# Modulation rows made by GpSimd as per-partition sums in the first block, summed by TensorE in the second

## The reference

```python
x = x + 0.5 * swiglu(rms_norm(x, norm_ffn1[l]), ffn1_in[l], ffn1_out[l])
...
x = x + 0.5 * swiglu(rms_norm(x, norm_ffn2[l]), ffn2_in[l], ffn2_out[l])
```

```python
m = jax.nn.silu(c) @ mod_w[l] + mod_b[l]            # 1024 x 6144 weights, for both layers
sh1, sc1, g1, sh2, sc2, g2 = jnp.split(m[:, None, :], N_MOD, axis=-1)
h = rms_norm_2(x, norm1_g[l]) * (1.0 + sc1) + sh1
mc = jax.nn.silu(c_ctx) @ mod_w[l] + mod_b[l]       # used in layer 0 alone, its first 2 x 1024 columns
```

## Time and profile before

| what | us |
|---|---|
| median of 3 runs | 3894.78 |
| the profiled execution, its own time | 3896.48 |
| its span in the trace | 3894.4 |
| first up stage (22.9 to 155.9) | 133.0 |
| first down stage (155.9 to 220.9) | 65.0 |
| modulation stage (1917.6 to 2128.6) | 211.0 |

### The profile page before, as it was taken

One profiled execution on the slowest core, in us unless ns is written; L12 is line 12 of the kernel. 1 busy time (PEld: TensorE's weight loads), 2 busy tenths in 40 slices (PEclk: granted clock), 3 DMA queues, 4 the chain that ended last, 5 costly groups with the idle time before them and its releaser, 6 DMA issues. The chain is left out here.

```text
span 3894.4 us, 51801 instructions
## 1 busy us (share of the span) xinstructions
PE 3014.0 (77%) x18986; PEld 2115.1 (54%) x18986; DVE 2191.8 (56%) x4138; ACT 1255.4 (32%) x2479; POOL 629.4 (16%) x544
## 2 busy tenths in 40 slices
PE   7988682798998786479887687677777776777776
PEld 7887671697988576369633557322222262222222
DVE  5455755553545566555300545777777457777774
ACT  3332112332433210333211233344444323444443
POOL 0000000000000000000011000444444204444442
PEclk9999895899999898589999758899999988999999
DMA  6453000444545200144585303899999838999997
GB/s 211 149 178 124 2 5 30 148 160 152 189 141 179 95 2 8 49 157 151 205 297 205 106 6 115 331 421 421 421 421 419 334 119 367 421 421 421 421 419 308
DMA packets 274498, 849.81 MB, mean 218 GB/s; under 512 B 13528, under 2 KB 161136, under 8 KB 208240
## 3 DMA queue, kind: packets, MB, share of 16 engines
q0 software_dynamic: 73728, 536.90, 33.2%
q1 hardware_dynamic: 200560, 310.19, 23.7%
HBM read 846.00 MB, written 1.05 MB: 218 GB/s over the span
## 5 line engine op out<-in xcount | busy, mean ns | idle before, releaser
L595 DVE TENSOR_TENSOR weight_parts_lo<-raw_weights,weight_parts_hi 128x512 fp32r<-128x512 f32 (+7 forms) x224 | 497.2, 2243 | 340.1 <-ACT weight_parts_hi L571 340.1
L571 ACT CAST weight_parts_hi<-raw_weights 128x512 fp32r<-128x512 f32 (+7 forms) x224 | 409.2, 1861 | 417.0 <-PE banks L450 367.8
L2226 PE MATMUL banks<-raw_weights,diagonals 128*128 128x512 f32 x832 | 414.1, 636 | 152.1 <-ACT diagonals L184 151.0
L448 PE MATMUL banks<-normedT_hi,weight_parts_hi 128*128 128x256 f32 x1664 | 478.1, 287 | 20.2 <-DVE weight_parts_lo L595 20.2
L2226 PE MATMUL banks<-expert_rows,diagonals 128*128 128x512 f32 x816 | 395.7, 624 | 115.3 <-ACT diagonals L184 114.5
L449 PE MATMUL banks<-normedT_lo,weight_parts_hi 128*128 128x256 f32 x1664 | 476.9, 287 | 0.0
L450 PE MATMUL banks<-normedT_hi,weight_parts_lo 128*128 128x256 f32 x1664 | 476.8, 287 | 0.0
L2226 PEld LDWEIGHTS banks<-raw_weights,diagonals 128*128 128x128 f32 x832 | 154.9, 199 | 407.9 <-ACT diagonals L184 231.8
L1640 POOL TENSOR_TENSOR modulation<-modulation,mod_bias 128x512 f32<-128x512 f32 x24 | 30.3, 1264 | 2087.3 <-DMA mod_bias<-mod_b 1953.2
L2138 POOL DMA_INDIRECT raw_weights<-peer_rows,expert_ids x208 | 242.8, 1167 | 749.3 <-DVE expert_ids L151 468.0
L2226 PEld LDWEIGHTS banks<-expert_rows,diagonals 128*128 128x128 f32 x816 | 149.8, 195 | 358.9 <-ACT diagonals L184 224.1
(11 more groups left out here) (391 smaller groups left out, 5081.1 us busy)
## 6 DMA issues: line engine op xcount, KB each, us to landing
raw_weights<-ffn_in SPq DMA_DIRECT2D x88, 1024.0 KB, 7.5
raw_weights<-mod_w SPq DMA_DIRECT2D x24, 2048.0 KB, 8.1
raw_weights<-ffn_out SPq DMA_DIRECT2D x44, 1024.0 KB, 4.9
raw_weights<-w_in SPq DMA_DIRECT2D x32, 1376.0 KB, 6.1
raw_weights<-peer_w_q SPq DMA_DIRECT2D x16, 1024.0 KB, 5.6
raw_weights<-w_branch SPq DMA_DIRECT2D x8, 1024.0 KB, 7.4
raw_weights<-w_out SPq DMA_DIRECT2D x8, 1024.0 KB, 5.0
raw_weights<-attn_in_w SPq DMA_DIRECT2D x4, 1792.0 KB, 7.2
```

The costliest lines, as they stand in the source:

```text
L448: nc.tensor.matmul(out, lhs.hi, rhs.hi, start=start, stop=False)
L571: nc.scalar.copy(parts.hi[:, u, cs], k.raw[:, u, cs]).then_inc(high, 1)
L595: nc.vector.tensor_tensor(parts.lo[:, u, cs], k.raw[:, u, cs], parts.hi[:, u, cs].bitcast(F32), ALU.subtract).then_inc(low, 1)
L2226: last = nc.tensor.matmul(k.bank(2 * j + half), diag[:, g % DIAGS, :], ring[g % RING][:, D + half * BANK:D + (half + 1) * BANK], start=t = ...
```

## The change

The modulation products leave the second block's first stage. Weights and conditions are laid out anew in DRAM, as `mod_tiles` (24 tiles to a layer, 128 partitions x 8 chunks x 256 columns, 1 MB) and `cond_columns` (128 x 16, both conditions as columns). The conditions are loaded in the program's first stage, and ACT takes their silu in its second.

In each of the first block's feed-forwards GpSimd takes a share of the layer's 24 side tiles. It multiplies each 256-column chunk by the condition's value on each partition and adds the eight products up (1024, 512 and 256 columns wide), so that one row of 256 sums is left on each partition. The first 8 tiles are done for both conditions. SP loads the side tiles and stores the sums to DRAM from its own stream, between the loads of the stage's weights. The shares: first feed-forward 5 tiles up and 3 down, all for both conditions; second 9 tiles up and 7 down, for one. Side tiles double-buffer in their own SBUF (`side_weights`), and the second condition's products lie in one buffer (`side_products`).

In the second block the modulation stage loads the sums (1 MB and 2 x 3 MB) and the broadcast biases (1 MB and 2 x 3 MB), sums over the partitions with a matrix of ones (28 float32 matmuls 128 x 512), and DVE adds each bank to the bias.

```diff
+class SideSums:
+    COLS = 256
...
+    def load(self, sp, i):
+        if i < len(self.which):
+            sp.dma_start(self.w[:, i % 2, :], self.tiles[self.which[i]]).then_inc(self.k.sem[f"side_in{i % 2}"], 16)
...
+    def step(self, sp, i):
+        if i >= len(self.which):
+            return
+        if i > 0:
+            sp.wait_ge(self.k.sem["side_out"], self.stores(i))
+            self.load(sp, i + 1)
+        sp.wait_ge(self.k.sem["side_done"], i + 1)
+        n = self.which[i]
+        cs = slice(n * self.COLS, (n + 1) * self.COLS)
+        sp.dma_start(self.sums[:, cs], self.w[:, i % 2, 0:self.COLS]).then_inc(self.k.sem["side_out"], 16)
+        if n < self.both:
+            sp.dma_start(self.ctx_sums[:, cs], self.other[:, 0:self.COLS]).then_inc(self.k.sem["side_out"], 16)
+    def end(self, sp):
+        sp.wait_ge(self.k.sem["side_out"], self.stores(len(self.which)))
+    def make(self, pool):
+        k, C = self.k, self.COLS
+        for i, n in enumerate(self.which):
+            pool.wait_ge(k.sem[f"side_in{i % 2}"], 16 * (i // 2 + 1))
+            w = self.w[:, i % 2, :]
+            places = [(self.other, KC), (w, 0)] if n < self.both else [(w, 0)]
+            if len(places) > 1 and i > 0:
+                pool.wait_ge(k.sem["side_out"], self.stores(i))
+            for to, first in places:
+                for kc_ in range(KC):
+                    k.nc.gpsimd.tensor_scalar(to[:, kc_ * C:(kc_ + 1) * C], w[:, kc_ * C:(kc_ + 1) * C],
+                                              k.cond[:, first + kc_:first + kc_ + 1], None, ALU.mult)
+            for width in (4 * C, 2 * C, C):
+                pool.drain()
+                for to, first in places:
+                    last = k.nc.gpsimd.tensor_tensor(to[:, 0:width], to[:, 0:width], to[:, width:2 * width], ALU.add)
+            last.then_inc(k.sem["side_done"], 1)
...
 def stream(...):
-        steps(sp, 2, tiles, load)
+        if side is None:
+            steps(sp, 2, tiles, load)
+        else:
+            side.load(sp, 0)
+            side.load(sp, 1)
+            for t in range(2, tiles):
+                load(t, t % 2, t // 2)
+                side.step(sp, t - 2)
         if ahead is not None:
...
+        if side is not None:
+            side.end(sp)
...
 def modulations(k, a, mods, cm, cx, ahead):
+        loads = [(first[:, 6 * D:], a["ctx_mod_sums"][0]), (cm[:, :], rows(a["mod_b_2"][0:1, 0:2 * D])),
+                 (first[:, 0:6 * D], a["mod_sums"][0]), (mods[0][:, :], rows(a["mod_b_2"][0:1, :])),
+                 (later[:, :], a["mod_sums"][1]), (mods[1][:, :], rows(a["mod_b_2"][1:2, :]))]
...
+                sp.wait_ge(S["summed"], 16)
+                preload(k, sp, ahead)
                 sp.wait_ge(S["written"], 16)
+            @block.tensor
...
+                for n, (src, dst) in enumerate(jobs):
+                    if n in (0, 4, 16):
+                        pe.wait_ge(S[f"part_in{(0, 4, 16).index(n)}"], 32)
+                    if n >= 8:
+                        pe.wait_ge(S["drained"], n - 7)
+                    nc.tensor.matmul(k.bank(n % 8), ones[:, :], src, start=True, stop=True).then_inc(S["summed"], 1)
...
+                for n, (src, dst) in enumerate(jobs):
+                    dve.wait_ge(S["summed"], n + 1)
...
+                    o.add(dst, dst, k.bank(n % 8), free=True).then_inc(S["drained"], 1)
```

More of the change, by code:

```diff
@@ L525, in preload, with __init__, stores @@
     k.preloaded = True
-def stream(k, block, wts, ahead, size, parts, done, done_per, finish_steps, act_steps=None):
+class SideSums:
+    COLS = 256
+    def __init__(self, k, tiles, sums, ctx_sums, which, both, room):
+        self.k, self.tiles, self.sums, self.ctx_sums, self.which, self.both = k, tiles, sums, ctx_sums, which, both
+        self.w, self.other = room
+    def load(self, sp, i):
+        if i < len(self.which):
+            sp.dma_start(self.w[:, i % 2, :], self.tiles[self.which[i]]).then_inc(self.k.sem[f"side_in{i % 2}"], 16)
+    def stores(self, i):
+        return 16 * sum(1 + (n < self.both) for n in self.which[:i])
+    def step(self, sp, i):
[29 more added lines that the diff above has]
+            last.then_inc(k.sem["side_done"], 1)
@@ L534, in stream @@
+def stream(k, block, wts, ahead, size, parts, done, done_per, finish_steps, act_steps=None, side=None):
     nc = k.nc
@@ L561, in _ @@
                 ahead.load(k, sp, t, t)
+        if side is not None:
+            side.end(sp)
+    if side is not None:
+        @block.gpsimd
+        def _(pool):
+            side.make(pool)
     @block.scalar
@@ L694, in finish_steps, with linear_turned_stage @@
                     finish(o, b // 2, b % 2, k.bank(b))
-        stream(k, block, wts, ahead, step * D, parts, used, 1, finish_steps)
+        stream(k, block, wts, ahead, step * D, parts, used, 1, finish_steps, side=side)
     k.clear()
-def linear_turned_stage(k, rhs, wts, halves, finish, pre=None, ahead=None):
+def linear_turned_stage(k, rhs, wts, halves, finish, pre=None, ahead=None, side=None):
     nc = k.nc
@@ L740, in act_steps, with swiglu @@
                 pre(o, t * 2 + s, v, k.bank(v)).then_inc(pre_done, 1)
[L742 removed]
+        stream(k, block, wts, ahead, size, parts, summed, 2, finish_steps, None if pre is None else act_steps, side)
     k.clear()
[L748 removed]
+def swiglu(k, gain, w_in, w_out, ahead, side_part):
     with ExitStack() as c:
+        size = KC * SideSums.COLS
+        room = k.sb("side_weights", [P, 2, size], ctx=c), k.sb("side_products", [P, size], ctx=c)
         hT = split_sb(k, "normedT", [P, KC, SEQ], c)
@@ L1575, in first_layer @@
         linear_sum_stage(k, mT, KC, w_mix, residual, w_up)
[L1576 to L1642, removed]
@@ L1645, in modulations @@
+    swiglu(k, row("norm_ffn2"), w_up, sum_weights(mat("ffn2_out"), NF), None, side(range(8, 17), range(17, 24)))
 def modulations(k, a, mods, cm, cx, ahead):
@@ L1658, in _ @@
             def _(sp):
[L1659 to L1662, removed]
+                for n, (dst, src) in enumerate(loads):
+                    sp.dma_start(dst, src).then_inc(S[f"part_in{n // 2}"], 16)
                 sp.dma_start(cx[:, :, :], a["ctx_2"][0].rearrange("(j p) d -> p j d", p=P)).then_inc(S["written"], 16)
+                sp.wait_ge(S["summed"], 16)
@@ L1666, in _ @@
             @block.vector
             def _(dve):
[L1668 to L1690, removed]
+                o = Ops(nc, dve, True)
+                nc.vector.memset(ones[:, :], 1.0).then_inc(S["stored"], 1)
+                for n, (src, dst) in enumerate(jobs):
+                    dve.wait_ge(S["summed"], n + 1)
+                    if n in (0, 4, 16):
+                        dve.wait_ge(S[f"part_in{(0, 4, 16).index(n)}"], 32)
+                    o.add(dst, dst, k.bank(n % 8), free=True).then_inc(S["drained"], 1)
@@ L2259, in _ @@
                         nc.vector.memset(lam[:, l, 1:2], 1.0 - init)
+                @block.scalar
+                def _(act):
+                    nc.scalar.activation(k.cond[:, :], k.cond[:, :], ACT.Silu)
             k.clear()
```

39 lines of the change are left out of this document (26 added, 13 removed).

## The result

The changed kernel takes 4275.32 us, the median of 4 runs (4272.76 to 4276.68), against 3895.2 (3894.43 to 3899.07): a ratio of 1.0973, 95% interval 1.0957 to 1.0989. It is slower by 380 us where 176 were forecast, and outside the range.

What follows compares the result with a forecast made beforehand. PE was taken to bound the modulation, up and down stages. From 3896.5 us, minus 157 (modulation), plus 2 (start), 317 (side work with exclusion) and 14 (cold restarts) gave 4072.5, less 1.7 for the median: 4071 us, range 3930 to 4170.

Steps and rivals of the forecast that it cites:

- the price of a multiplication: GpSimd's side tiles: a 128x256 multiplication by a per-partition value takes 0.45 us, between 0.24 and 0.63; eight take 3.6.
- the forecast's 5 for VectorE's lost turns: Second up stage: 5 us added for VectorE's turn lost to a running GpSimd add.
- The modulation stage: Second block's first stage: falls from 211 to 54 us, bounds 45 and 75, a gain of 157 us.
- the 2 us forecast: Program's start: a silu with its table load stands alone and a small load, costing 2 us.
- SP as the point: Feed-forward stages: SP's wait for side tiles makes GpSimd's pace the weights' pace; 198 us over two layers without exclusion.
- The exclusion: Feed-forward stages: GpSimd stands still while VectorE reads two SBUF tensors, raising the side work's cost from 198 to 317 us.
- some up to 7: Sign of exclusion: POOL adds of 128x1024 mostly take 2.5 us, some up to 7 when the 4.43 us subtraction falls on them.
- No exclusion: Rival: the gather's surplus is something of its own, so VectorE does not hold GpSimd; 3952 us, chance 0.14.
- the faster kernel: Rival: in the first feed-forward GpSimd keeps up, with a cycle of 15.5 us; 3852 us, chance 0.09.
- The expensive modulation stage: Rival: bias rows at half the rate and sums at 1.2 GHz make the new stage 100 us; 4117 us, chance 0.05.
- the hidden work: Rival: SP's waits for side tiles never end last in the feed-forwards; around 3740 us, chance 0.02.

Runs made afterwards that it cites:

- e2: Changed kernel with GpSimd's eight multiplications a set made one 128x2048 tensor-by-tensor multiplication with the condition broadcast, same result: 4064.8 us, 211 less.
- e1: Changed kernel without side loads, GpSimd work and stores, its new modulation stage kept: 3731.4 us, 165.2 less than the kernel before.
- e4: Changed kernel with SP's steps of the side work put behind later weight loads or at the stage's end, same arithmetic: 4065.5 us, 211 less.
- e5: Changed kernel with VectorE's weight_parts_lo copying one SBUF tensor instead of subtracting two, output another: 4114.2 us, 162 less.
- e6: Changed kernel with both the one wide multiplication a set and SP's later steps, at somewhat other places, same result: 3904.8 us.

## Why the prediction was wrong

**The step that failed** is the price of a multiplication: "I take 0.45, about the middle", between 0.24 and 0.63. It takes 0.90 us. The upper end was wrong as an end: it took for granted that an instruction which reads one tensor costs no more than the add, which reads two. Its work by the element is 2.5 ns, where the adds pay 2.1 to 2.3 (2.34 us for 1024, 0.72 for 256). Put through the prediction's own steps, a set is 11.9 us and the cycle of a tile for both conditions 27.6. First up comes to 5.5 + 5 x 27.6 - 3.9 + 26 + 15.5 + 46.1 + 1.8 = 229 us (231.6 measured); first down to 5.5 + 82.8 - 3.9 + 7 + 9.1 + 32.6 + 1 = 134 (135.2); second up, at 11.9 + 5.3 a tile, to 5.5 + 8 x 17.2 + 28.8 = 172, with the forecast's 5 for VectorE's lost turns 177 (172.7); second down, at 14.2, to 5.5 + 99.4 + 21 = 126 (131 and 129.0). Against 133, 65, 133 and 65 that is 270 us a layer, and 3896.5 - 162.7 + 0.1 + 540 + 14 = 4288, where the profiled execution took 4276.5. The 11 us left hide small misses that partly cancel. In second up SP's stores follow each other after 20.4 and 12.2 us in turn, as two splits fall on one side tile and none on the next: 16.3 in the mean for 17.2. What comes after the eighth takes 33.1 us for 28.8. e2 is the same check from the other side.

**The modulation stage.** 48.3 us for the forecast 54, a gain of 162.7 for 157. At the program's start the 2 us forecast came to 0.1: the first norm starts 1.5 us later, but the table load that stood at its head is now ahead of it, and the first up stage starts at 23.0 us for 22.9. e1 gives 165.2 for the 162.6 of both. Of the 2.6 between, 2.4 lie at the loop's turn: in e1 the norm of layer 1 starts there without a table load of 1.28 us, 4.4 us after the start of VectorE's last add in place of 6.7.

**SP as the point.** Right, and shown: the loads of the first up stage lie 31 us apart, and e4, which only moves SP's waits, gains 211 us.

**The exclusion.** Right for GpSimd, and shown by e5 for the second input in SBUF. The forecast's terms for it were 317 - 198 = 119 us; e5 took 162 off. The difference lies in second up, where 15 was forecast and e5 gains 37 in layer 0: at the true price nothing of a side tile's cycle hides under PE's 11.5 us, so that every split counts in full. That VectorE stands still as well the forecast left out, but for those 5 us. It shows in the changed kernel itself, at the add that the forecast had named as the sign, "some up to 7" us. No add of 128x1024 took more than 2.46. The split that began under one waited for it:

```profile
964.19 2.40 POOL L580 TENSOR_TENSOR side_weights<-side_weights 128x1024 f32<-128x1024 f32 x1
...
965.23 5.65 DVE L665 TENSOR_TENSOR weight_parts_lo<-raw_weights,weight_parts_hi 128x4096 fp32r<-128x4096 f32 x1 [3.78 <-ACT weight_parts_hi L641]
```

The add ends at 966.59, and 4.42 us undisturbed from there would end at 971.01; the split ends at 970.88. The holding of GpSimd fell on others: 34 of its 512 multiplications (up to 5.17 us) and 20 of its 64 adds of 128x512 (up to 5.30). So whichever begins first holds the other, and the Trainium skill (SBUF — State Buffer, Who interferes with whom), by which either side can hold the other, agrees with these rows and with e6. For the time of this kernel it mattered little: a split of 4096 took 4.67 us in the mean against 4.43, and all 107 splits of 4096 and 2048 columns lost 23 us, in stages where PE mostly waited for the weights.

**Rivals.** No exclusion (3952) and the faster kernel (3852) fall with e5 and with the 0.90 us. The expensive modulation stage (4117) falls with its 48.3 us, the hidden work (around 3740) with the 231.6 us of first up. The Trainium skill (GPSIMD Engine Reference, Engine selection) calls one-input work roughly line-rate; for this form the runs don't agree. With a per-partition scalar 256 columns took 0.90 us and 2048 took 5.44.

**The range** was too narrow for a reason that could be seen: one price stood for 496 instructions on the path (62 sets of eight), each 0.1 us of it being worth 50 us, and no row showed it. The neighbours' rows were taken for bounds. Its ends are also not the sums they are said to be: 3965 - 9 is 3956 and 4159 + 21 is 4180, where 3960 and 4175 stand, and the range ends at 4170. None of these reaches 4275.

## What to carry to other kernels

An idle engine is not a free one: ask what it shares with the busy one, and who waits for it in whose queue. A wait for slow side work in the queue that feeds the bound engine makes the side work's pace the stage's pace; put it behind the loads that it doesn't concern. Here the same sums, fused on VectorE, cut into pieces that fit its gaps and with SP's steps two weight tiles later, turned a loss of 380 us into a gain of 153 (3744.2 against 3897.5).

## What was not expected of the hardware

- GpSimd's `tensor_scalar` with a per-partition scalar costs more than its `tensor_tensor`: 5.44 us for 128x2048, against 3.60 for a product with a broadcast second operand, and 2.34 for an add of 128x1024.
- That product with a broadcast operand, 1.76 ns an element, is also cheaper by the element than an add of two full tensors, 2.28.
- VectorE's fused multiply-and-add of 128x256, one of a dependent chain, took 0.54 us (2.16 for four), where GpSimd needs 0.90 for the multiplication alone.
